# Storing gates in smaller pieces over more slots of a streaming pass: 16 x 512 KB instead of 8 x 1 MB, with a shorter selection stage

## What is computed

```python
def peer_ffn(x, w_pq, sub_keys, expert_u, expert_v):
    q = (x @ w_pq).reshape(bsz, seq, PEER_HEADS, 2, PEER_KEY_DIM)
    scores = jnp.einsum('bshcd,hcnd->bshcn', q, sub_keys)
    top_v, top_i = lax.top_k(scores, PEER_TOPK)              # 16 of 128, 8 heads x 2 halves
    cand = top_v[..., 0, :, None] + top_v[..., 1, None, :]    # pairs of the two halves
    ...
    best_v, best_pos = lax.top_k(cand, PEER_TOPK)             # 16 experts a head, 128 a token
    gate = jax.nn.softmax(best_v, axis=-1)
    def block(args):                                          # for 128 tokens at a time
        xt, it, gt = args
        h = jax.nn.gelu(jnp.einsum('ted,td->te', expert_u[it], xt))
        return jnp.einsum('te,ted->td', gt * h, expert_v[it])
```

## Time and profile before

| | |
|---|---|
| median of three runs | 3925.08 us |
| the profiled execution's own time | 3924.02 us |
| its span in the profile | 3922.3 us |
| TensorE matmul busy | 3442.4 us, 88% |
| VectorE busy | 2989.1 us, 76% |
| ScalarE busy | 1478.1 us, 38% |
| GpSimd busy | 1093.0 us, 28% |
| DMA, mean over the span | 214 GB/s, 840.08 MB |
| tile loads of the expert streams | 512 of 512 KB, 5.7 us from issue to landing |
| stores of gates | 48 of 1024 KB, 10.4 us from issue to landing |
| stores of hidden values | 256 of 192 KB, 6.0 and 5.4 us |
| gathers of `expert_u` rows | 256, GpSimd busy 363.1 us |

### The profile page before, as it was taken

The page is one execution under the profiler, slowest core; times in us unless marked ns, Lnnn a source line. Parts: engine busy times, 40 slices in busy tenths (PEclk is TensorE's granted clock), DMA queues, the critical chain, the costliest instruction groups (busy, mean ns, idle before and its releaser), DMA issues.

```text
span 3922.3 us, 57979 instructions
## 1 busy us (share of the span) xinstructions
PE 3442.4 (88%) x19870; PEld 1971.8 (50%) x19870; DVE 2989.1 (76%) x5160; ACT 1478.1 (38%) x1972; POOL 1093.0 (28%) x748
## 2 busy tenths in 40 slices
PE   7778987988887889999886889879888888899997
PEld 3334643555454546666542346435454545566664
DVE  5887535798888868888848865358989897688887
ACT  4314432335353533333342144233353535333333
POOL 1640000041313224444326300001413131344443
PEclk9889998999999999999998899999999999999998
DMA  4000312486969599999640003124869696999995
GB/s 170 22 0 11 129 49 86 143 281 220 327 210 334 204 374 371 371 389 372 232 136 12 0 22 129 43 94 166 289 227 318 222 319 215 382 370 375 386 367 199
DMA packets 385870, 840.08 MB, mean 214 GB/s; under 512 B 32576, under 2 KB 231232, under 8 KB 384960
## 3 DMA queue, kind: packets, MB, share of 16 engines
q1 hardware_dynamic: 311424, 564.60, 40.9%
q0 software_dynamic: 73728, 268.47, 18.5%
q10 hardware_dynamic: 576, 5.37, 0.3%
HBM read 731.36 MB, written 106.95 MB: 214 GB/s over the span
## 4 chain that ended last, share of the span: by engine, by line
PE 28%; DVE 11%; issue 3%; DMA 3%; ACT 2%; SPq 2%; POOL 1%; DVEq 0%; ACTq 0%; POOLq 0%
PE ps L1582 4%; PE ps L1584 4%; PE ps L1583 4%; PE ps L116 3%; PE ps L118 3%; PE ps L117 3%; DVE wl L95 2%; DMA wf<-experts 2%; DVE xT L1741 1%; SPq L82 1%; PE ps L592 1%; DMA xT<-urows,small 1%; ACT wh L89 1%; PE ps L152 1%; DVE small L1706 0%
## 5 line engine op out<-in xcount | busy, mean ns | idle before, releaser
L116 PE MATMUL ps<-xh,wh 128*128 128x384 f16 (+1 forms) x2880 | 1004.8, 349 | 211.3 <-DVE wl L95 63.4
L95 DVE SCALAR_TENSOR_TENSOR wl<-wf,wh 128x1024 f16<-128x1024 f32 x656 | 804.2, 1227 | 435.3 <-ACT wh L89 420.5
L89 ACT ACTIVATE wh<-wf 128x1024 f16<-128x1024 f32 x656 | 690.9, 1054 | 1042.2 <-PE ps L1584 591.7
L117 PE MATMUL ps<-xl,wh 128*128 128x384 f16 (+1 forms) x2880 | 1002.8, 348 | 0.0
L118 PE MATMUL ps<-xh,wl 128*128 128x384 f16 (+1 forms) x2880 | 1001.4, 348 | 0.0
L1681 POOL DMA_INDIRECT xT<-urows,small x256 | 363.1, 1418 | 1168.5 <-DVE xT L1741 883.8
L1582 PE MATMUL ps<-work,wh 128*128 128x384 f16 x2048 | 667.7, 326 | 6.9 <-DVE work L1866 5.1
L1584 PE MATMUL ps<-work,wl 128*128 128x384 f16 x2048 | 667.6, 326 | 0.0
L1583 PE MATMUL ps<-work,wh 128*128 128x384 f16 x2048 | 667.6, 326 | 0.0
L1689 POOL DMA_INDIRECT work<-experts,small x256 | 448.7, 1753 | 583.4 <-DVE work L1875 558.0
L116 PEld LDWEIGHTS ps<-xh,wh 128*128 128x128 f16 x2880 | 286.9, 100 | 473.2 <-ACT work L1624 102.4
(11 more groups left out here) (334 smaller groups left out, 4317.1 us busy)
## 6 DMA issues: line engine op xcount, KB each, us to landing
wf<-experts SPq DMA_DIRECT2D x512, 512.0 KB, 5.7
wf<-proj SPq DMA_DIRECT2D x144, 512.0 KB, 3.3
gates<-work SPq DMA_DIRECT2D x48, 1024.0 KB, 10.4
work<-hid SPq DMA_DIRECT2D x256, 192.0 KB, 4.4
work<-gates SPq DMA_DIRECT2D x256, 192.0 KB, 5.3
hid<-work SPq DMA_DIRECT2D x192, 192.0 KB, 6.0
hid<-small SPq DMA_DIRECT2D x64, 192.0 KB, 5.4
xsave<-xT ACTq DMA_DIRECT2D x2, 2048.0 KB, 6.9
```

The lines of the kernel that those rows point to most:

```text
L89: m.nc.scalar.activation(m.wh[:, slot, :], m.wf[:, k, :], ACT.Copy, scale=WS).then_inc(m.high_done, 1)
L95: m.nc.vector.scalar_tensor_tensor(m.wl[:, slot, :], m.wf[:, k, :], WS, m.wh[:, slot, :], ALU.mult, ALU.subtract).then_inc(m.split_done, 1)
L116: m.nc.tensor.matmul(out, wh[:, k, :], xh[:, k, 0:n], start=(k == order[0]), stop=False)
L117: m.nc.tensor.matmul(out, wh[:, k, :], xl[:, k, 0:n], start=False, stop=False)
```

## The change

```diff
-R_SEL = 5
+R_SEL = 4
 R_CHUNK = 2
 R_PICK = 1
 R_TOK = R_SEL + 2 + R_CHUNK
 R_U = EB // RING
 ST_N = NT - 1
 R_LAST = R_U - R_PICK - ST_N * R_TOK
-STORES = 8
+STORES = 16
...
+def storing(j):
+
+    at = j - R_PICK * RING
+    return at >= R_TOK * RING and at % (R_TOK * RING) < STORES
+
+
 def dots_by(j):
 
-    room = [min(1.8, max(0.0, 5.6 - other_work(i))) for i in range(EB)]
+    room = [min(1.1 if storing(i) else 1.9, max(0.0, 5.6 - other_work(i))) for i in range(EB)]
     return int(sum(room[:j]) * N_SEL / sum(room) + 0.5)
```

## The result

The changed kernel takes 3904.07 us (median of 5 runs, 3899.58 to 3906.45) against 3922.63 us (3922.57 to 3931.66) of the kernel before in the same session. The ratio of the mean times is 0.9946, with a 95% interval of 0.9931 to 0.9960, so it is 0.54% faster. The forecast was 3926, no change. The profiled execution took 3904.07 us (span 3902.3), 20.0 us less span than before.

A forecast was written before the change was run, and what follows sets the result against it. VectorE was taken to bound selections, picks and turns, DMA the tail. Per layer -5.7 - 54.2 + 1 + 19.7 + 40 = +0.8, layer two +0.5, both +1.3 us: forecast 3926 us, range 3896 to 3952.

The forecast's parts named there:

- the likeliest case: Whole run: the forecast itself, no change, 3926 us, own range 3916 to 3937; chance 0.44.
- Selection 1: First selection stage of the first pass: four splits and one product fewer on VectorE, -5.7 us a layer.
- Selections 2 and 3: Selection stages carrying stores: 82.8 us each without stall, -54.2 and -54.5 a layer, plus 1 for remaining stalls.
- Picks with turns: Stages after each selection: denser products wait for the ring of four gathered rows, 44.5 us, +19.7 a layer.
- The tail: Last slots of the first pass, 16 before, 28 after: taken as DMA's, +40 us a layer, ends +28 and +53.
- the drained rate: About 410 GB/s, at which a backlog without stores is drained; by it the longer tail costs +39 us.
- My end for that case, +28: Tail with everything hidden behind TensorE: 28 slots at 3.90 us, 109.2 us, +28.0 a layer.
- The fixed cost: About 2 us on each DMA: 24 more stores, an estimated 48 us a layer; rival at 4043, chance 0.02.
- The stores' issues: SyncE's queue: each added store is an issue of 0.43 us beside its waits for splits, cost 0.
- the faster rival: Stores smooth, rows cheap: rows +13.1, tail +35, stalls 0, -11.8 us a layer, 3901 us; chance 0.28.
- The slower rival: Slots 100 to 127: storing slots at 5.4 us by DMA, tail +53, +13 a layer, 3952 us; chance 0.22.
- the stall did not stay: Rival: half stores still hold back loads in both storing selections, +17.5 us a layer, 3961 us; chance 0.04.

The follow-up runs named there:

- e2: The changed kernel without its rule for products: room 1.8 in every slot. 3890.42 us, ratio 0.9910 to the kernel before.
- e4: The kernel before, with stores of token tiles 1 and 2 in 16 pieces of 512 KB, tile 3 as before. 3893.70 us, ratio 0.9915.
- e1: The kernel before with selections of 16 slots instead of 20, stores still 8 of 1 MB. 3918.70 us, ratio 0.9983.
- e5: The kernel of e2 with 8 stores of 1 MB, one in every second slot, instead of 16 of 512 KB. 3896.69 us, ratio 0.9923.
- e9: The changed kernel with a ring of five gathered rows instead of four. 3897.49 us, ratio 0.9926 to the kernel before.
- e11: The changed kernel with token tile 3, in the tail, stored as before, 8 of 1 MB in 8 slots. 3909.51 us, ratio 0.9959.
- e3: The changed kernel with stores as before, 8 of 1 MB in the first 8 slots after a spread. 3929.30 us, ratio 1.0008.
- e8: The kernel of e2 with each 512 KB store written in runs of 4 KB instead of 512 bytes. 3887.31 us, ratio 0.9897.

## Why the prediction was wrong

The miss is 10.9 us in layer one and 7.1 in layer two. The value lies inside the stated range of 3896 to 3952 only because that range took in the rivals; the likeliest case's own, 3916 to 3937, missed it. By its own steps:

1. **Selection 1** was 2.2 us a layer better than -5.7. The missing 2.1 are the waits of the earlier trace rows: before, slot 4 had no selection step, and VectorE ran ahead and waited for ScalarE's half of the next two tiles. Now every slot has a step, and the wait is gone. The prediction listed these waits and then left them out of its term. The sum of prices without the wait is 92.0, the measured length.
2. **Selections 2 and 3** came at 82.9 and 83.0 against 82.8 without and 83.3 with the stall that I had added. The stall went whole. My condition (DMA demand below what the queue moves) held: 347 GB/s in the windows. e2 and e4 show how much room there was: 352 and 368 GB/s with next to no stall. e1 says that a part of the stall (5 to 6 of 9 us) would have gone with 16-slot selections alone; e2 and e5 say that the rest goes by spreading.
3. **Picks with turns** were forecast at 44.5. Layer one had 42.0, 44.4, 43.4, layer two 44.1, 42.8, 44.7, mean 43.6. The mechanism is as described: in turn 2 a product starts 8.6 us after the fourth before it ended, and VectorE's waits for rows there were
```profile
DVE xT L1747 <- DMA xT<-urows,small: 4.6, 4, 1.6
```
   where I had 5.4 in three. Over all six stages these waits are 2.8 to 5.4, 4.2 on average, so the size was about 1 us a tile too large. e9 shows that the ring is one limit, and its timeline that GpSimd's pace is another, which I did not have.
4. **The tail** is the step that failed: +40 against +35.6 and +35.1, which is 4.4 of the 10.9 us missed in layer one and 4.9 of 7.1 in layer two, and outside the 119 to 124 us that I had named as the sign of being right. I took the tail as bound by DMA, priced what the twelve slots bring at the drained rate and left the stall of the sixteen as it was. With the stores of before that is nearly right: e11 gives 120.6 and 118.6, so +39.4 and +37.5, e1 +42.8 for its three more products. What I left out is what spreading does to a stage that is bound by TensorE in some slots and by DMA in others: it moves bytes from the second kind into the first, and TensorE's waits fell from 11.1 us to 1.2, which is nearly all that there was to gain. (e11 changes spacing and size together; e1, e5 and e2 give the spacing 1.7 and 4.1 us of a tail, the size 2.1 and 0.3.) My end for that case, +28, was wrong too. It took the 18.8 us of 81.2 beyond sixteen slots of TensorE as waits, but TensorE had begun the second pass after 75.3 us, so only 12.9 were; with all of them gone its end moves by 46.8 - 12.9 = 33.9 us, and 34.3 and 33.9 were measured. e11 accounts for 3.8 of the 4.4 us and for 2.4 of the 4.9; the rest in layer two is open.

   The fixed cost that the Trainium skill (DMA: Bandwidth & Descriptors, Anatomy of one DMA) puts on each DMA did not show. The page fits it on DMAs that GpSimd issues, and these stores are issued by SyncE. With 24 more stores a layer, e2's storing stages are all shorter than those of e1.
5. **The stores' issues**, 0.43 us at the median in selection 2 and 2.57 at most, lengthened no stage, as said.

The sum was a difference of large terms (-60 and +60 a layer) and its four misses had one sign. In the measured sum the faster rival (3901, tail +35, no stall) is nearly what happened, but for its cheap rows: those cost 16.2 and 18.3 us a layer, between its 13.1 and the forecast's 19.7 and nearer to the latter. Its +35 had no working behind it, so that it was right is luck.

What the prediction did not ask is which part of the change helps. Spreading the stores is the gain (e1 0.9983 to e2 0.9910; e3 1.0008 to the change's 0.9946; e4 0.9915 alone). Shorter selections are nearly neutral (0.9983), and the rule for products costs about 0.36% (0.9946 against 0.9910), since it moves nine products a layer into stages where each costs 1.9 us. The slower rival, a tail of 125 us or more, did not come; the stall did not stay.

## What to carry to other kernels

Spread a large transfer over as many slots of a streaming loop as its deadline allows before cutting anything else: in the selections here it was the spacing that counted and not the size of a piece, in the tail both, and in slots that compute paces there is DMA time that a burst of stores leaves unused. A stage in which single slots are bound by different engines must be summed slot by slot, both for what is added and for what is already stalled. Work out the floor of the busiest engine from that engine's own start and end, not from the marks of another that runs ahead of it. Work that takes only 1.15 us on VectorE costs more where its operands come through a short ring: before moving it, look at how long a buffer takes to come back and how many are asked for in that time.

## What the runs showed of the hardware

- With 16 slots of 512 KB or with 1 MB in every second slot the DMA engines carry loads, gathers and stores in a selection at 347 to 368 GB/s with VectorE delayed by at most 1.4 us (e4); DMA share reads 1.01 to 1.02 there. In the changed tail it reads 1.00 to 1.07 while TensorE hardly waits. A share of 1 did not mean that the stage was bound by DMA.
- A load behind a 1 MB store was held at issue for 6.05 us in e5's selection 2, and VectorE, which paces the stage, did not wait.
- In e11's tail the granted clock fell to half twice, for 3.4 us each, after TensorE had waited; the next waits were shorter by about as much (0.43 and 0.26 us against 2.07 to 2.44).
- The same bytes stored in 4 KB runs instead of 512 bytes (e8 against e2) raise the tail from 392 to 405 GB/s.
- In turn 2 of e9, with VectorE at work throughout, GpSimd issued gathers of 128 rows of 4 KB one in 2.29 us (1.98 each). In the same two stages of the changed kernel single ones took 0.94 to 3.04 us. Why the length varies was not tried.
